# Seven block products in place of eight in the down projections of a decoder layer's FFN

## The reference

```python
h = rmsnorm(x, ffn_norm)
g = jnp.einsum('bsd,df->bsf', h, w_gate)
u = jnp.einsum('bsd,df->bsf', h, w_up)
x = x + jnp.einsum('bsf,fd->bsd', jax.nn.silu(g) * u, w_down)
return rmsnorm(x, final_norm)
```

## Time and profile before

| | us |
|---|---|
| median of 3 runs | 301.22 |
| span of the profiled execution | 298.3 |
| TensorE matmuls busy | 290.9 (98%) |
| TensorE weight loads busy | 238.3 (80%) |
| VectorE busy | 204.0 (68%) |
| ScalarE busy | 164.7 (55%) |
| GpSimd busy | 18.9 (6%) |

### The profile page before, as it was taken

One profiled execution on the slowest core, in us unless ns is written; L12 is line 12 of the kernel. 1 busy time (PEld: TensorE's weight loads), 2 busy tenths in 40 slices (PEclk: granted clock), 3 DMA queues, 4 the chain that ended last, 5 costly groups with the idle time before them and its releaser, 6 DMA issues.

```text
span 298.3 us, 4426 instructions
## 1 busy us (share of the span) xinstructions
PE 290.9 (98%) x1432; PEld 238.3 (80%) x1432; DVE 204.0 (68%) x337; ACT 164.7 (55%) x279; POOL 18.9 (6%) x25
## 2 busy tenths in 40 slices
PE   8999999999999999999999999999999999999992
PEld 4788888888888888888888888888888888888881
DVE  3888999998998779638565645556374656454354
ACT  4878569664886459645364544453543635454224
POOL 0011000000123306000000000000000000000010
PEclk9999999999999999999999999999999999999998
DMA  7999517797877636867858484766747474841003
GB/s 247 403 421 363 204 30 243 214 287 242 237 209 211 270 118 207 245 219 247 298 176 274 156 288 151 244 204 190 260 116 285 127 287 138 285 152 27 0 0 141
DMA packets 31228, 62.77 MB, mean 210 GB/s; under 512 B 3952, under 2 KB 17264, under 8 KB 31088
## 3 DMA queue, kind: packets, MB, share of 16 engines
q1 hardware_dynamic: 29056, 61.03, 61.4%
q10 hardware_dynamic: 2160, 1.59, 1.8%
HBM read 55.72 MB, written 1.11 MB: 191 GB/s over the span
## 4 chain that ended last, share of the span: by engine, by line
PE 93%; DMA 2%; issue 1%; DVE 1%; ACT 1%; SPq 0%; POOL 0%; POOLq 0%; ACTq 0%; DVEq 0%
PE bank L482 30%; PE bank L484 29%; PE bank L483 29%; PE bank L559 2%; DMA room<-in_first 2%; PE bank L509 1%; PE bank L532 1%; PE bank L492 1%; PE bank L535 0%; DVE xs L1193 0%; PE bank L536 0%; PE bank L537 0%; SPq L389 0%; ACT rot L963 0%; DVE w_lo L1004 0%
## 5 line engine op out<-in xcount | busy, mean ns | idle before, releaser
L765 ACT ACTIVATE w_hi<-raw 128x1024 fp32r<-128x1024 f32 x94 | 97.8, 1055 | 82.6 <-PE bank L484 72.7
L976 DVE TENSOR_TENSOR w_lo<-raw,w_hi 128x1024 fp32r<-128x1024 f32 x94 | 111.7, 1213 | 16.2 <-ACT w_hi L765 14.9
L482 PE MATMUL bank<-w_hi,x_hi 128*128 128x512 f32 x270 | 106.5, 394 | 0.4 <-DVE w_lo L1004 0.4
L484 PE MATMUL bank<-w_hi,x_lo 128*128 128x512 f32 x270 | 105.2, 389 | 0.0
L483 PE MATMUL bank<-w_lo,x_hi 128*128 128x512 f32 x270 | 105.2, 389 | 0.0
L482 PEld LDWEIGHTS bank<-w_hi,x_hi 128*128 128x128 f32 x270 | 50.7, 188 | 12.1 <-DVE w_lo L1004 0.9
L484 PEld LDWEIGHTS bank<-w_hi,x_lo 128*128 128x128 f32 x270 | 50.7, 188 | 10.6
L483 PEld LDWEIGHTS bank<-w_lo,x_hi 128*128 128x128 f32 x270 | 50.7, 188 | 10.1
L482 PE MATMUL bank<-w_hi,h_hi 128*128 128x512 f32 (+1 forms) x82 | 31.6, 385 | 0.0
L484 PE MATMUL bank<-w_hi,h_lo 128*128 128x512 f32 (+1 forms) x82 | 31.5, 384 | 0.0
L483 PE MATMUL bank<-w_lo,h_hi 128*128 128x512 f32 (+1 forms) x82 | 31.5, 384 | 0.0
(11 more groups left out here) (96 smaller groups left out, 235.1 us busy)
## 6 DMA issues: line engine op xcount, KB each, us to landing
raw<-in_weights SPq DMA_DIRECT2D x94, 512.0 KB, 5.1
room<-room SPq DMA_DIRECT2D x76, 64.0 KB, 2.2
room<-in_first SPq DMA_DIRECT2D x3, 384.0 KB, 4.9
room<-in_first SPq DMA_DIRECT2D x1, 1024.0 KB, 8.5
xs<-in_x SPq DMA_DIRECT2D x2, 512.0 KB, 9.6
rot<-turned_sums SPq DMA_DIRECT2D x8, 128.0 KB, 4.0
room<-room ACTq DMA_DIRECT2D x12, 64.0 KB, 2.5
out<-rot SPq DMA_DIRECT2D x3, 256.0 KB, 2.0
```

Source lines behind the costliest of these rows:

```text
L482: pe.matmul(dst, a_hi, w1, start=first, stop=False)
L484: return pe.matmul(dst, a_lo, w1, start=False, stop=last)
L765: act.activation(w_hi[:, slot:slot + 2, :], raw[:, slot:slot + 2, :], ACT.Copy).then_inc(hi_ready, 1)
L976: dve.tensor_tensor(w_lo[:, slot:slot + 2, :], raw[:, slot:slot + 2, :], w_hi[:, slot:slot + 2, :].bitcast(f32), ALU.subtract).then_inc(lo ...
```

## The change

For chunks 0 to 9, the chunk's hidden matrix (256 tokens by 256 features) and its down weights (256 by 1024) are each taken as 2 x 2 blocks and multiplied with seven block products instead of eight (Strassen's method in Winograd's form). Four sums of weight blocks (P, Q, R, S, made by `down_sums` in three VectorE operations, one of them 128x1024) and four sums of hidden blocks (`hidden_sums`, three operations) are formed first. The seven products have a bank each and collect all ten chunks; `PRODUCTS` says which sums each multiplies, `PRODUCT_BANK` its bank. They are combined into the four output blocks once, at the end: by VectorE, and by GpSimd for two of them. Chunk 10 is multiplied plainly, on top of the banks.

With seven banks taken, gate and up have one bank (`GU_BANK`) from chunk 2 on: the half s = 0 is made, ScalarE copies silu(gate) and up out (`evacuate`), and then s = 1 is made in the same bank. TensorE makes the products in two groups: `down_first` (four products, forms A: raw blocks B11, B21, B22, P) at the end of a step and `down_second` (three, forms B: Q, R, S) in the middle of the next, between the two halves of gate and up. Both groups' high and low parts lie in the same tiles `down_hi` and `down_lo`, one after the other. Down blocks come in one DMA of 1 MB; gate/up pairs go through eight slots, two chunks ahead. The FFN loops are unrolled on all engines. Some tiles of the attention part share room with others (`qkT_first` with `vals`, `junk` with `probs`, `rotary` with `front`), with no change to its instructions.

```diff
+RAW_B12, RAW_B11, RAW_B21, RAW_B22, RAW_P, RAW_Q, RAW_R, RAW_S = range(8)
+H_A11, H_A22, H_A12, H_G, H_E, H_F, H_H = range(7)
+X_A21, X_A11, X_A22, X_A12 = range(4)
+FORMS_A, FORMS_B = range(RAW_B11, RAW_P + 1), range(RAW_Q, RAW_S + 1)
+PRODUCTS = {1: (H_A11, RAW_B11), 2: (H_A12, RAW_B21), 3: (H_H, RAW_B22), 4: (H_A22, RAW_S),
+            5: (H_E, RAW_P), 6: (H_F, RAW_R), 7: (H_G, RAW_Q)}
+PRODUCT_BANK = {1: 0, 2: 1, 5: 2, 3: 3, 7: 6, 6: 7, 4: 5}
+GU_BANK = 4
...
+            def down_blocks(c):
+                if c == 0:
+                    sp.wait_ge(valued, SC_TILES)
+                    sp.wait_ge(ot_lo, 2 * SH)
+                    sp.wait_ge(o_squared, 2 * SH)
+                else:
+                    sp.wait_ge(down_lo_ready, 2 * c - 1)
+                    sp.wait_ge(w_sum, 3 * c)
+                q = (STEP1 + c * STEP_BLOCKS + GU_BLOCKS) // QUAD
+                sp.dma_start(down_raw[:, 0:QUAD, :].rearrange("p b n -> p (b n)"),
+                             weights[q - FIRST_QUADS, :, :]).then_inc(in_down, 16)
...
+            for j in range(G_PAIRS):
+                gate_up_pair(1, j)
+            down_blocks(0)
+            for j in range(G_PAIRS):
+                gate_up_pair(2, j)
...
+            def step(c):
+                place_squares(c - 1)
+                if c + 2 < NCH:
+                    gate_up_pair(c + 2, 0)
+                    gate_up_pair(c + 2, 1)
+                    gate_up_pair(c + 2, 2)
+                if c < NCH - 1:
+                    down_blocks(c)
+                if c + 2 < NCH:
+                    gate_up_pair(c + 2, 3)
+            for c in range(1, NCH):
+                step(c)
...
-            def gate_up(k, s, slot):
...
-                if s == SH - 1:
-                    ins.then_inc(blk_done, 1)
-                elif k == KT - 1:
-                    ins.then_inc(gu_half, 1)
+                w1, w2 = gate_up_at(c, k, 1)
+                dst = bank[GU_BANK + s if c < 2 else GU_BANK]
+                ins = three_products(dst[:], x_hi[:, k, cols], x_lo[:, k, cols], w1[:, 0, :], w2[:, 0, :],
+                                     k == 0, k == KT - 1)
+                if k == KT - 1:
+                    ins.then_inc(gu_done, 1)
...
+            def product(c, n, w1, w2):
+                h, _ = PRODUCTS[n]
+                return three_products(bank[PRODUCT_BANK[n]][:], h_hi[:, c % 2, h, :], h_lo[:, c % 2, h, :], w1, w2,
+                                      c == 0, c == NCH - 2 and n not in (2, 3, 4))
+            def down_first(c, order=(1, 2, 5, 3)):
+                pe.wait_ge(down_lo_ready, 2 * c + 1)
+                pe.wait_ge(ht_lo, 2 * c + 2)
+                for n in order:
+                    at = PRODUCTS[n][1] - FORMS_A[0]
+                    ins = product(c, n, down_hi[:, at, :], down_lo[:, at, :])
+                ins.then_inc(down_done, 1)
+            def down_second(c, order=(7, 6, 4)):
+                pe.wait_ge(down_lo_ready, 2 * c + 2)
+                for n in order:
+                    if c == 0 and n == 4:
+                        pe.wait_ge(evacuated, 4)
+                    at = PRODUCTS[n][1] - FORMS_B[0]
+                    ins = product(c, n, down_hi[:, at, :], down_lo[:, at, :])
+                ins.then_inc(down_done, 1)
...
+                c = NCH - 2
+                pe.wait_ge(down_lo_ready, 2 * c + 2)
+                pe.wait_ge(ht_lo, 2 * c + 2)
+                for n in (6, 7):
+                    at = PRODUCTS[n][1] - FORMS_B[0]
+                    product(c, n, more_hi[:, at, :], more_lo[:, at, :]).then_inc(part_done, 1)
+                for n in (1, 5):
+                    at = PRODUCTS[n][1] - FORMS_A[0]
+                    product(c, n, down_hi[:, at, :], down_lo[:, at, :]).then_inc(part_done, 1)
...
+                turn_last_hidden()
+                for n in (2, 3):
+                    at = PRODUCTS[n][1] - FORMS_A[0]
+                    product(c, n, down_hi[:, at, :], down_lo[:, at, :])
+                at = PRODUCTS[4][1] - FORMS_B[0]
+                product(c, 4, more_hi[:, at, :], more_lo[:, at, :])
+                pe.wait_ge(lo_ready, STEP1_PAIR + (NCH - 1) * G_PAIRS + 2)
+                pe.wait_ge(last_lo, 1)
...
+            for h in range(2):
+                for s in range(SH):
+                    if h == 0:
+                        pe.wait_ge(evacuated, s + 1)
+                    gate_up_half(1, s, h)
             pe.wait_ge(res_done, 8)
-            step(1, first=True)
-            with pe.Fori(2, NCH - 1) as c:
+            down_first(0)
+            def step(c):
+                pe.wait_ge(evacuated, 2 * c if c > 2 else 3)
+                for h in range(2):
+                    gate_up_half(c, 0, h)
+                down_second(c - 2)
+                pe.wait_ge(evacuated, 2 * c + 1)
+                for h in range(2):
+                    gate_up_half(c, 1, h)
+                if c < NCH - 1:
+                    down_first(c - 1)
+                else:
+                    last_downs()
+            for c in range(2, NCH):
                 step(c)
-            step(NCH - 1, last=True)
...
+            def evacuate(c, s):
+                if c == 0 and s == 0:
                     act.wait_ge(rstd_ready, rstd_count["ffn"])
-                for s in halves:
-                    act.wait_ge(*((blk_done, done) if s else (gu_half, c + 1)))
-                    if not first:
-                        act.wait_ge(hid_ready, c * 2 + (s - 1))
-                    act.activation(silu[:, s, :], bank[4 + s][:, 0:FC], ACT.Silu,
-                                   scale=rstd[:, 6 + s:7 + s]).then_inc(silu_done, 1)
+                    act.wait_ge(valued, SC_TILES)
+                act.wait_ge(gu_done, 2 * c + s + 1)
+                if c and s == 0:
+                    act.wait_ge(hid_ready, c)
+                src = bank[GU_BANK + s if c < 2 else GU_BANK]
+                act.activation(silu[:, s, :], src[:, 0:FC], ACT.Silu, scale=rstd[:, 6 + s:7 + s])
+                act.activation(up[:, s, :], src[:, FC:2 * FC], ACT.Copy,
+                               scale=rstd[:, 6 + s:7 + s]).then_inc(evacuated, 1)
...
             def hidden_hi(c):
-                act.wait_ge(in_h, c * 16 * JS + 16 * JS)
-                act.activation(hidden[0], placed, ACT.Copy).then_inc(ht_hi, 1)
+                act.wait_ge(in_h, (c + 1) * 16 * JS)
+                if c >= 2:
+                    act.wait_ge(down_done, 2 * c - 2)
+                act.activation(h_hi[:, c % 2, H_A11:H_A12 + 1, :].rearrange("p x (i b) -> p x i b", b=SQ),
+                               placed[:, X_A11:X_A12 + 1, :, :], ACT.Copy).then_inc(ht_hi, 1)
...
+            def hidden_sums_hi(c):
+                act.wait_ge(h_sum, 3 * c + 3)
+                act.activation(h_hi[:, c % 2, H_G:H_H + 1, :].rearrange("p x (i b) -> p x i b", b=SQ),
+                               h_sums, ACT.Copy).then_inc(ht_hi, 1)
+            def down_first_hi(c):
+                act.wait_ge(w_sum, 3 * c + 1)
+                act.wait_ge(*((down_done, 2 * c) if c else (blk_done, FFN0)))
+                act.activation(down_hi, down_raw[:, FORMS_A[0]:FORMS_A[-1] + 1, :], ACT.Copy).then_inc(down_hi_ready, 1)
+            def down_second_hi(c):
+                act.wait_ge(w_sum, 3 * c + 3)
+                if c < NCH - 2:
+                    act.wait_ge(down_done, 2 * c + 1)
+                    to = down_hi
+                else:
+                    act.wait_ge(gu_done, 2 * c + 2)
+                    to = more_hi
+                act.activation(to[:, 0:len(FORMS_B), :], down_raw[:, FORMS_B[0]:FORMS_B[-1] + 1, :],
+                               ACT.Copy).then_inc(down_hi_ready, 1)
+            def last_down_hi(j):
...
+            gate_up_hi(1, 2)
+            gate_up_hi(1, 3)
+            evacuate(0, 0)
+            evacuate(0, 1)
             act.dma_start(gain_out, final_norm.partition_broadcast(P)).then_inc(in_gout, 16)
...
+            def step(c):
+                if c > 1:
+                    down_second_hi(c - 2)
+                if c < NCH - 1:
+                    gate_up_hi(c + 1, 0)
+                    gate_up_hi(c + 1, 1)
                 hidden_hi(c - 1)
-                for m in range(1, 4):
-                    split(m)
-                gated(c, c * STEP_BLOCKS + (STEP1 - STEP_BLOCKS + GU_BLOCKS), False)
-                split(4)
-                split(5)
-            with act.Fori(1, NCH - 1) as c:
-                step(c, 6)
-            step(NCH - 1, PAIRS - HI0 - (NCH - 2) * STEP_BLOCKS // 2)
+                hidden_sums_hi(c - 1)
+                if c == 1:
+                    down_first_hi(0)
+                evacuate(c, 0)
+                if c > 1:
+                    down_first_hi(c - 1)
+                if c < NCH - 1:
+                    gate_up_hi(c + 1, 2)
+                    gate_up_hi(c + 1, 3)
+                else:
+                    down_second_hi(c - 1)
+                    last_down_hi(0)
+                    last_down_hi(1)
```

(79 more changed lines are left out.)

283 lines of the change are left out of this document (141 added, 142 removed).

## The result

The changed kernel takes 323.62 us (median of four, 323.05 to 324.30) against 300.97 us in the runs beside it (300.71 to 301.33): ratio 1.0753, 95% interval 1.0734 to 1.0771. It is slower by 22.6 us. The forecast was 316.2 us with a range of 304.5 to 321.5, so the sign held and the size did not.

A forecast was written before the change was run, and what follows sets the result against it. The prediction took TensorE, busy 98% of the span, to bound the kernel. Its terms, -5.4 + 6.8 + 2.0 + 10.6 + 1.0 = +15.0 us on a profiled 298.3 us, plus 2.9 us to the median, gave 316.2 us, range 304.5 to 321.5.

The forecast's parts named there:

- The saving, -5.4: TensorE in the FFN: 24 fewer matmuls before output block (0, 0) is complete, at 0.2267 us each, -5.4 us.
- VectorE and ScalarE by the column: Wide operations priced on a line: VectorE 0.17 + 0.00102 us per column, ScalarE 0.17 + 0.00086.
- The fourth rival: Columns beyond 1024 cost half, first landing takes 4.0 us, TensorE bounds the steps; 300.0 us in total, chance 0.08.
- The loop, +10.6: Chain from one down_first to the next, through down_hi: 16.97 us against TensorE's 15.64, eight rounds, +10.6 us.
- the second rival: Squares land late in every step: at 6.5 us the loop grows by 0.6 a round; 321.0 in total, chance 0.15.
- The first wait, +6.8: Before down_first(0): TensorE asks at 133.9 and can start at 140.7, after landing and a series of work; +6.8 us.
- With the same 5.9 us of landing: Chunk 0's hidden squares, sent at 125.6, land after 5.9 us as in the kernel before, at 131.5.
- The clock, +2.0: After the 6.8 us wait TensorE falls to half clock: ten matmuls at 0.42 us, not 0.2267; +2.0 us.
- The first rival: The clock holds through the wait before down_first(0); 314.2 us in total, chance 0.15.
- The end, +1.0: Last step: down low parts late by 0.65, hidden transpose by 0.15, VectorE's combination by 0.2; together +1.0 us.
- The third rival: Only the wait before down_first(0) counts, the loop having unseen slack; 305.1 us in total, chance 0.09.
- 17.6 or more with ScalarE idle for a DMA: Sign in the steps: at 17.6 us or more, ScalarE idle for a DMA before hidden rounding, landings are the cause.

The follow-up runs named there:

- e7_combined: Changed kernel with ScalarE and VectorE queues reordered, last down pairs loaded in step 9, two warm matmuls before down_first(0), GpSimd's second wide addition later; 298.51 us, 0.9929 of before.
- e1: Changed kernel with each chunk's three weight sums cut to 8 columns, so its output is not the layer's; 322.31 us.
- e4: Changed kernel with the same instructions, ScalarE's and VectorE's queues put in another order in every step; 301.01 us, ratio 1.003 to the kernel before.
- e3: Changed kernel with SyncE sending the hidden squares ahead of the fourth gate/up pair and loading the last two down pairs in step 9; 318.60 us.
- e2: Changed kernel with 36 matmuls on warm data filling TensorE's wait ahead of down_first(0); 319.60 us.
- e10: Changed kernel with GpSimd's second wide addition at the end waiting for VectorE's sixth combination instead of its fourth; 322.41 us.

## Why the prediction was right in sign and short by 7.4 us

By the prediction's own steps, against the measured 22.9. Three terms of its sum were too small: the loop by 4.4 us, the first wait by 2.4 and the end by 1.0; the clock was 0.3 too large, and 0.45 is the attention part of this execution. That is 7.9 on the spans, and 7.4 on the medians, since the profiled execution lay 2.9 below the median before and 2.4 after.

- **The saving, -5.4.** Held. With the order changed TensorE runs 15.64 us a step without a wait, and e7_combined ends 2.4 us under before; the other 3.0 must lie in its first wait and its end, by subtraction.
- **VectorE and ScalarE by the column.** Held: 1.76 and 2.29 us on VectorE for 1536 and 2048 columns (1.73 and 2.26 taken), 1.49 and 1.92 on ScalarE (1.50 and 1.94). The Trainium skill (VectorE: DVE Perf Modes, section on the TRN2 errata) gives 2.29 us for 2048 columns, and the trace agrees. The fourth rival, cheap wide operations, falls. "Busy time alone would just fit. The order does not" is what e1 and e4 show.
- **The loop, +10.6.** This is the largest miss: 15.0. The loop and its links were right, but its length was 17.30 and not 16.97: I priced down_first at full pitch, and behind a wait it takes 0.2 more until the next engine can go on; with 0.13 of small ones that is 0.33 x 8 = 2.6. The landings, which the sum put at nothing, added 0.21 x 8 = 1.7. That is the second rival, on top of the forecast, at a third of its price. The waits came at the two places named, with 0.6 for the evacuation, but only 0.43 to 0.49 of idle time for the A low part; an idle time in the trace is not its whole cost: 0.60 and 0.43 of idle stand for 17.30 - 15.64 = 1.66 us, since each is counted from the modelled end of a matmul, 0.16 us after the next would have started, and the first matmul behind it holds the second up by 0.11; that is most of the difference.
- **The first wait, +6.8.** 9.2. The chain behind the landing was 9.4 against 9.2. The step that failed there is "With the same 5.9 us of landing": it was 8.3, which is 2.4 more. I carried the landing of before over, and bounded it by the worst seen, 5.9 plus 0.7, though the change puts more in the queue ahead of it; e3 and e7, with 1 MB less ahead, get it down to 6.4 and to 5.8 or less. The squares went out 0.3 later than I had it and the chain was 0.2 longer, and against that TensorE was ready 0.45 later.
- **The clock, +2.0.** Held: 1.7 by the row, 1.6 by e2. The first rival falls. The waits of 0.4 to 1.2 us left the clock at 1.00, as said.
- **The end, +1.0.** About 2.0. The wait of 0.62 at 301.95 is the 0.65 named. Not foreseen is the 0.77 that VectorE lost beside GpSimd. I priced GpSimd's 128x512 at 1.8 us and called it covered (it took 1.3); what counted was that it ran at the same time. Undoing that gave 0.3 to 0.4 back (e10); what makes up the rest of the 2.0 was not separated.
- **The third rival**, only the first wait counts, falls with the rounds.
- **The signs.** TensorE at 91% (92 said), waits at the places said. "17.6 or more with ScalarE idle for a DMA" was to mean landings. Rounds reached that in two of eight, and ScalarE idled for the DMA in seven; but it idles so at 17.30 too (1.66 us in the round of e2 above), where the landing costs nothing. That sign did not tell the two apart; e3 did. VectorE was busy for 82% of the rounds (101.4 of 122.9 us) and not for about 90%: the forecast added whole durations, and instructions back to back overlap by 0.1 us each.

What stays open: why landings in the rounds vary from step to step and between executions, 5.5 to 6.1 us from issue to use in e2 and 5.6 to 6.7 in the changed kernel, when SyncE issues the same work; and whether e2's undisturbed rounds come from the filling or by chance. A double buffer for the down forms, which would break both loops through it by space and not by order, was not tried.

## What to carry to other kernels

When a change fills the room of two in-order engines, do not add up busy time: write down, for each instruction that waits, what stands behind it in its queue, and follow the chain until it comes back to itself; then cut that link and look for the next loop, since the second was only 0.3 us shorter here, and a one-link repair would have looked like proof that order does not matter. Where two groups take turns in one buffer, follow both handovers: the first loop came from B forms that waited for down_first, the second from A forms that waited for down_second. Work that needs no transfer (weight sums) is better queued ahead of work that waits for one; here that showed only in the rounds with a late landing, and was not tested alone. And take a transfer's landing not from where it stood before, but with the bytes that the change puts ahead of it.

## What the hardware showed beyond that

A VectorE instruction with two SBUF inputs that started during a GpSimd addition of SBUF tiles was held until that was through: it ended 0.54 us (309.86 to 309.32) after GpSimd's in the changed kernel and 0.55 (310.69 to 310.14) in e10, though it had started 0.37 us after GpSimd's in the one and 0.76 in the other. VectorE instructions with a PSUM source beside the GpSimd additions took 0.68 or 0.69 as always. The Trainium skill (SBUF — State Buffer, section SBUF: two separate sides) says that a VectorE instruction with two SBUF inputs and a GpSimd one that reads SBUF take turns on a shared port pair, which the first holds for its whole instruction. The traces agree.

TensorE's clock: behind waits of 3.2, 7.3 and 9.2 us the granted clock was 0.50 when matmuls began again or fell to it just after, behind waits of 2.4 us and less in the traces of the steps it stayed at 1.00. In the steps of the changed kernel the first matmul behind a wait took 0.50 us, not 0.39, and the second started 0.34 later, not 0.23.
